# Modulations in column tiles, paired attention heads, and state-space parameters computed inside the mixture, in a whole-model kernel on one core

## The chip, the cores and the metric

One core of a Trainium2 chip runs the whole kernel in one launch. The metric is the device time of an execution in microseconds (us), and the figure given is the median over several executions. The engines are named as in the profile: PE is TensorE (PEld its weight load), DVE is VectorE, ACT is ScalarE, POOL is GpSimd, SP is SyncE, which only issues the transfers of the weights.

## The reference

The input is 256 tokens of width D = 1024, in fp32, and a conditioning vector `c` of D numbers. Everything below is computed in fp32 or in split fp32 products. Cut to what matters here:

```python
# first block, layer 0 (forgetting attention) and layer 1 (latent attention)
c_act = silu(c)
for layer in range(2):
    sh1, sc1, g1, sh2, sc2, g2 = split(c_act @ w_mod[layer] + b_mod[layer], 6)     # 6 x 1024 numbers
    h = rmsnorm(x, g) * (1 + sc1) + sh1
    mix = forgetting_attention(h) if layer == 0 else latent_attention(h, shared_kv)
    x = x + g1 * mix
    h = rmsnorm(x, ffn_norm_g) * (1 + sc2) + sh2
    x = x + g2 * grouped_moe(h)              # 16 experts, 2 of them per token
    if layer == 0: shared_kv = mla_shared_kv(x, c_act, ...)   # with 2 x 1024 modulations of its own
x = rmsnorm(x, final_norm_g)
# forgetting attention: 16 heads of 64
log_f = log_sigmoid(h @ w_f + b_f); cum = cumsum(log_f)
s = q k^T / 8 + cum[query] - cum[key]; p = softmax(causal(s)); o = p v
# second block
xn = rmsnorm(x, norm1_g)
u, q, k, v, qi, ki, wi, g_ssm, g_attn = split(xn @ w_in)
# state space, 32 groups x 64 states, 16 channels a group
dt = exp(log_dt); a_bar = exp(lam * dt); b_bar = (a_bar - 1) / lam * b
state[t] = a_bar * state[t-1] + b_bar u[t];  y = Re(c state) + d_skip * u
y_ssm = gelu(y); y_ssm = y_ssm * sigmoid(y_ssm @ w_glu)
y_attn = attention over the 64 keys with the highest index score (qi, ki, wi) of each query
x = x + (sigmoid(g_ssm) * (y_ssm @ w_ssm_up) + sigmoid(g_attn) * (y_attn @ w_attn_up)) @ w_out
x = x + peer_ffn(rmsnorm(x, norm2_g));  out = rmsnorm(x, norm_f_g)
```

## The kernel before

Each engine has one instruction stream in a fixed order, written out by hand; semaphores tie them together. Tokens lie in two chunks of 128 partitions (`C = 2`). There is no planner; what runs when is the order in which each stream is written.

**Weights.** SP loads the dense weights as slabs of 1024 rows by 512 columns (2 MB) into a ring of three (L505 to L545); the load of slab r waits until slab r-3 is released. `stream` (L172) lists the slabs and cuts them into pieces of at most 512 columns. `gemm` (L727) multiplies one piece after another; `gemm3` (L700) does it for the pieces of `stream_cut`, whose weights ACT and DVE first split into a high and a low part (`highs`, `lows`), three products for each. In the mixture of experts (MoE) the ring holds units of 512 KB, freed by `moe_low`, the count of DVE's low parts.

**Modulations.** `c_act` lies as a column `cT[:, k]` for each of 8 blocks of 128. For a piece of 512 modulations, `gemm` multiplies (L751) the column, broadcast to 128 x 128, with the 128 x 512 weights, 8 times, so that the sum stands on every partition; DVE adds the bias, which lies broadcast in `MOD` (`add_bias`, L1381). The 6144 modulations of layer 0 (`mod0`, 12 pieces) come first in the program, ahead of everything else. Their bias (3 MB broadcast) is loaded on ACT's queue, ahead of X. The modulations of the shared KV and the first two parts of layer 1 are summed on DVE during MoE 0 (`mod_part_of`, L1612, into the accumulators `ACC`), and after it PE adds them over the partitions and adds the bias (L944 to L960), in 32 matmuls of 256 columns, two kinds alternating: one with the bias rows (L956), one with `ones` (L958). Only then is the KV norm's gain loaded by POOL. The other parts of layer 1 (`mod1_a` to `mod1_e`) are `gemm` pieces between the projections.

**Attention A** (L758 to L822 on PE, L1448 on DVE). A step is four heads of one chunk of queries, eight steps in all. For every head PE multiplies q and k (L779, 64 rows) and adds `-cum[key]` with a second matmul of 16 rows (L781, a broadcast column of the identity against `NCT`). DVE adds the mask and takes the maximum, ACT the exponential, DVE normalizes, PE transposes (L794) and multiplies with v (L808).

**State space and attention C.** After layer 1 DVE computes two norms (`rms`, L1351), then the state-space parameters (L1736 to L1795, on 128 x 16 tiles), the powers `POW`, the rotary rotation of the attention C projections (L1797) and the phase tables for b = 0 (`first_phases`, L1804): powers of `a_bar/|a_bar|` for 256 steps, by doubling. The 16 states' tiles are done in four rounds b = 0..3 (L1819 to L1849): PE makes `bu` (L995), DVE rotates by the phases, scans 8 times, and rotates back. POOL makes the phase tables of b = 1, 2, 3 (L613 to L636), those of 2 and 3 after the states of the round two before, as they share two buffers. PE does `c_u` (the u projection), `c_p` (q, k, v, index) and then, between the rounds, `c_g` (four pieces, the gates). The outputs y5 of the state space (L1009, L1011) are taken in token layout: DVE adds `d_skip * u`, ACT does the gelu, PE transposes, then `glu`, the product, and a second transpose. Only after this come the index scores (L1029), the top-64 selection (L1867 to L1888) on DVE, attention C, `ssm_up` and `attn_up`. The small inputs of the state space (27 transfers on POOL's queue, L599 to L610) are issued between layer 1's attention and its experts.

After the merge come the output projection and the product-key experts (PEER), which the change leaves alone.

## Time and profile before

| | before |
|---|---|
| median of 3 runs | 2576.05 us |
| runs | 2576.4, 2576.05, 2563.88 us |
| profiled execution, its own time | 2567.64 us |
| its span | 2565.7 us |
| mean granted clock of PE | 0.862 |
| instructions | 22185 |
| read from memory | 609.69 MB |
| busy share | PE 80%, DVE 58%, PEld 52%, ACT 32%, POOL 24% |

The span runs from the first to the last instruction of the profiled execution; 1.94 us of its time lie outside. A busy share says how long an engine had an instruction under way, not that it set the end. All positions below (as "at 201 us") are from the span's start. In a row of the chain of waits the first number is the start, the second the duration; the chain is the work that ended last, followed back from the last instruction.

### The profile page before, as it was taken

How to read it: one execution, taken by the hardware profiler on the slowest of the kernel's cores; microseconds unless marked ns; L12 is line 12 of the kernel's file. 1: busy time of each engine (PE TensorE's matmuls, PEld its weight loads, DVE VectorE, ACT ScalarE, POOL GpSimd, SP SyncE). 2: the span in 40 equal slices, each digit the busy share in tenths (PEclk: the TensorE clock that was granted, in tenths of full speed). 3: DMA queues.
4: the chain of work that ended last, by engine and by line, in shares of the span. 5: the costliest groups of instructions: out<-in, count | busy, mean ns of one | idle time of the engine just before them, and what ended most of it. 6: DMA issues, size and time to landing. Idle time of an engine off the chain costs nothing.

```text
span 2565.7 us, 22185 instructions
## 1 busy us (share of the span) xinstructions
PE 2052.1 (80%) x7651; PEld 1342.8 (52%) x7651; DVE 1500.0 (58%) x2516; ACT 827.9 (32%) x1266; POOL 611.1 (24%) x749
## 2 busy tenths in 40 slices
PE   5999779999998886999993876488177767677777
PEld 2495568888745665788882444358133223233223
DVE  1243567899843456558994674534675556475642
ACT  0043234588713433447881100223121112121110
POOL 0000000000000003000000363000556666666663
PEclk9995779999979987999997976688588888888788
DMA  8740058999944407669983301031789999999996
GB/s 315 271 166 0 1 206 294 328 388 375 348 156 158 176 33 149 206 204 353 379 334 135 134 20 70 33 131 58 288 334 363 372 381 355 376 372 359 369 382 254
DMA packets 193711, 617.46 MB, mean 241 GB/s; under 512 B 18968, under 2 KB 21328, under 8 KB 193088
## 3 DMA queue, kind: packets, MB, share of 16 engines
q1 hardware_dynamic: 114336, 325.98, 35.3%
q0 software_dynamic: 78704, 285.11, 30.0%
q10 hardware_dynamic: 560, 4.96, 0.5%
q8 instruction: 61, 1.00, 0.2%
q14 instruction: 50, 0.41, 0.0%
HBM read 609.69 MB, written 6.29 MB: 240 GB/s over the span
## 4 chain that ended last, share of the span: by engine, by line
PE 63%; DVE 11%; issue 10%; POOL 7%; DMA 4%; ACT 2%; another core or an unknown queue 1%; SPq 0%; DVEq 0%; ACTq 0%; POOLq 0%
PE PS L882 16%; PE PS L1056 13%; PE PS L903 8%; PE PS L719 5%; PE PS L751 5%; PE PS L738 4%; PE PS L710 4%; POOL peer_rows L654 2%; PE PS L779 2%; POOL peer_rows L665 1%; DVE AR L1326 1%; POOL AR L665 1%; PE PS L781 1%; DVE peer_rows L1963 1%
## 5 line engine op out<-in xcount | busy, mean ns | idle before, releaser
L1963 DVE SCALAR_TENSOR_TENSOR peer_rows<-peer_rows,PS 128x1024 f32<-128x1024 f32 x256 | 311.5, 1217 | 143.5 <-DMA peer_rows<-in_peer_u,MOD 124.1
L1609 DVE TENSOR_TENSOR weights_low<-ring,weights_high 128x1024 fp32r<-128x1024 f32 x231 | 278.9, 1223 | 79.8 <-ACT weights_high L1158 77.3
L1056 PE MATMUL PS<-peer_rows,HT 128*128 128x512 f32 x376 | 193.5, 654 | 125.5 <-ACT HT L1314 77.2
L1158 ACT ACTIVATE weights_high<-ring 128x1024 fp32r<-128x1024 f32 x231 | 242.9, 1061 | 121.2 <-PE PS L882 76.0
L654 POOL DMA_INDIRECT peer_rows<-in_peer_u,MOD x256 | 242.2, 946 | 151.2 <-DVE MOD L1953 73.4
L1609 DVE TENSOR_TENSOR weights_low_more<-ring,weights_high_more 128x1024 fp32r<-128x1024 f32 x153 | 185.3, 1223 | 46.6 <-ACT weights_high_more L1158 44.9
L1056 PEld LDWEIGHTS PS<-peer_rows,HT 128*128 128x128 f32 x376 | 76.5, 208 | 239.5 <-issue 158.7
L1491 DVE TENSOR_TENSOR weights_low<-ring,weights_high 128x1024 fp32r<-128x1024 f32 (+1 forms) x81 | 96.4, 1198 | 158.4 <-ACT weights_high L1080 158.1
L562 POOL DMA_DIRECT2D expert_rows<-HT x10 | 5.4, 543 | 768.2 <-ACT HT L1180 768.2
L1158 ACT ACTIVATE weights_high_more<-ring 128x1024 fp32r<-128x1024 f32 x153 | 161.1, 1061 | 72.2 <-PE PS L882 44.6
L882 PE MATMUL PS<-weights_high,slots_high 128*128 128x512 f32 x386 | 156.2, 405 | 10.1 <-DVE weights_low L1609 10.1
L665 POOL DMA_INDIRECT peer_rows<-in_peer_v,MOD x148 | 140.7, 951 | 88.3 <-issue 37.8
L751 PE MATMUL PS<-ring,cT 128*128 128x512 f32 x320 | 144.4, 613 | 21.6 <-DMA ring<-in_w_mod 20.5
L1080 ACT ACTIVATE weights_high<-ring 128x1024 fp32r<-128x1024 f32 (+1 forms) x81 | 83.1, 1040 | 236.4 <-DMA ring<-in_a_w_in 100.1
L1308 ACT ACTIVATE MOD<-MOD 128x16 f32<-128x16 f32 x16 | 3.4, 216 | 481.5 <-DVE peer_rows L1963 244.3
L882 PE MATMUL PS<-weights_low,slots_high 128*128 128x512 f32 x386 | 154.2, 400 | 0.0
L882 PE MATMUL PS<-weights_high,slots_low 128*128 128x512 f32 x386 | 154.1, 399 | 0.0
L1056 PE MATMUL PS<-AR,HT 128*128 128x512 f32 x216 | 115.8, 672 | 42.7 <-issue 39.5
L1056 PE MATMUL PS<-peer_rows,AR 128*128 128x512 f32 x216 | 113.2, 659 | 45.0 <-issue 42.6
L738 PE MATMUL PS<-ring,HT 128*128 128x512 f32 (+3 forms) x320 | 120.9, 540 | 1.4 <-ACT HT L1071 1.4
L665 POOL DMA_INDIRECT AR<-in_peer_v,MOD x108 | 102.6, 950 | 80.4 <-remote 42.3
L1056 PE MATMUL PS<-AR 128*128 128x512 f32 x216 | 107.2, 645 | 15.8 <-issue 14.0
(356 smaller groups left out, 4077.4 us busy)
## 6 DMA issues: line engine op xcount, KB each, us to landing
ring<-in_exp_w_gate SPq DMA_DIRECT2D x128, 512.0 KB, 5.7
ring<-in_exp_w_up SPq DMA_DIRECT2D x128, 512.0 KB, 5.7
ring<-in_exp_w_down SPq DMA_DIRECT2D x128, 512.0 KB, 5.5
ring<-in_w_mod SPq DMA_DIRECT2D x20, 2048.0 KB, 8.3
ring<-in_w_in SPq DMA_DIRECT2D x7, 2048.0 KB, 8.6
ring<-in_a_w_in SPq DMA_DIRECT2D x6, 2048.0 KB, 7.8
ring<-in_kv_w_mod SPq DMA_DIRECT2D x16, 512.0 KB, 5.0
ring<-in_w_mod SPq DMA_DIRECT2D x16, 512.0 KB, 5.2
```

The costliest lines, as they stand in the source:

```text
L654: pool.indirect_dma_start(out=u_row(k), out_offset=None, in_=A["peer_u_2"][0], in_offset=bass.IndirectOffsetOnAxis(ap=EXPERT[:, c, PT_ * h ...
L665: pool.indirect_dma_start(out=v_row(k), out_offset=None, in_=A["peer_v_2"][0], in_offset=bass.IndirectOffsetOnAxis(ap=EXPERT[:, c, PT_ * h ...
L710: last = nc.tensor.matmul(PS[:, pair + j // 2, o:o + T], ws[a][:, k, :], tokens[b][:, k, :], start=i == 0, stop=i == len(steps) - 1)
L719: last = nc.tensor.matmul(PS[:, pair + c, 0:n], tokens[b][:, 2 * j + k, P * c:P * c + P], ws[a][:, k, :], start=j == 0 and k == 0 and i == ...
L738: last = nc.tensor.matmul(PS[:, pair + c, 0:n], lhs[:, k, P * c:P * c + P], w[:, k, off:off + n], start=k == 0, stop=k == s["kb"] - 1)
L751: last = nc.tensor.matmul(PS[:, pair, 0:n], cT[:, k:k + 1].to_broadcast((P, P)), w[:, k, off:off + n], start=k == 0, stop=k == s["kb"] - 1)
L882: last = nc.tensor.matmul(PS[:, (0 if kind == "G" else 2) + i, :], (XTH, XTL)[b][:, 2 * q + k, P * tile:P * tile + P], w[a][:, DE * k:DE * ...
L903: last = nc.tensor.matmul(PS[:, y_bank(r, ti) + half, :], hidden[b][:, q, P * i:P * i + P], w[a][:, 512 * half:512 * half + 512], start=j ...
L1056: last = nc.tensor.matmul(PS[:, 4 + 2 * c + half, :], diagonal(k), v_row(k)[:, 512 * half:512 * half + 512], start=h == 0 and j == 0, stop ...
L1158: A_(high_of(n0 + n), raw(ring_slot(layer, m)), ACT.Copy).then_inc(S("moe_high"), 1)
L1609: V.tensor_tensor(low_of(n0 + n), raw(ring_slot(layer, ring_no[layer, "E", n])), high_of(n0 + n).bitcast(fp32), ALU.subtract).then_inc(S(" ...
L1963: V.scalar_tensor_tensor(u_row(k), u_row(k), 1.0, PS[:, 2 * c:2 * c + 2, :].rearrange("p a k -> p (a k)"), ALU.mult, ALU.mult, accum_out=D ...
```

## The change

1. **Modulations in column tiles.** The column is broadcast to 128 x 32 only, and the 8 blocks are placed in turn in four column tiles of 32, so that a partial sum of two blocks stands on each quarter of the partitions. ACT copies them to `PARTS` (`mod_copies`), one matmul with `ones` (128 x 128 against 128 x 512) adds them over the partitions, 32-fold, and DVE adds the sum times 1/32 to the bias in `MOD` (`add_mod`). The partial products of piece i+1 are issued ahead of the total of piece i.
2. **Modulations of layer 0 in four parts.** `mod0_a` (4 pieces) and `mod0_b` (1) come before `a_qk`; `mod0_c` (5) after `a_v` and the cumulated sums, before attention A; `mod0_d` (2) after `a_o`. The bias's last 2 MB are loaded by POOL; X comes ahead of the bias on ACT's queue; the statistics of the first norm are taken before the modulations arrive.
3. **Paired heads in attention A.** The forget piece (16 columns) is the first of `a_v`. `Fn`/`NCT` stand twice, at rows 0 and 64, and the bias matmul has 64 rows, in the same half as its head; the order is q·k of the even head, q·k of the odd head, bias even, bias odd, so that successive matmuls alternate between row halves.
4. **Sums after MoE 0.** POOL puts the bias on partition 0 of the accumulators before MoE 0, and PE adds them in 8 matmuls of 512 columns.
5. **State-space parameters in MoE 1.** The same small DVE operations are cut into some 23 steps; one follows each of DVE's expert units from n = 19 on. ACT's exponentials and sines stand at n = 18 and n = 24 of its own units, the first behind a wait for all 27 transfers, which POOL issues once `moe_low` is past 12 units of layer 1. POOL then makes small phase tables (16 steps near, 16 steps far; operations of at most 256 elements a partition), and, after it has gathered the expert rows and the weight stages are free, the full tables of all four b, each of 6 operations on 128 x 1024. `n1`'s gain has a place of its own, `MOD[:, 0:D]`.
6. **State-space order.** `c_u` and `glu` are computed transposed, which takes away three sets of transposes; outputs are 32-column tiles side by side; the skip is a per-partition scalar (`skip`); the rotation stands after round b = 1; the index scores and the top-64 stand ahead of `glu`'s product, and `ssm_up` and the fourth gate piece (`c_h`) ahead of attention C.

```diff
-        gemm("mod0", None, ("c_act", 1))
+        gemm_mod("mod0_a")
+        gemm_mod("mod0_b")
         tp("h_a", ...)
         gemm("a_qk", None)
         gemm("a_v", HT)
...
+        gemm_mod("mod0_c")
         tp("cum", ("negcum", 1))
         attention("A", ...)
         gemm("a_o", None)
+        gemm_mod("mod0_d")
...
+            def partial(g, r, off, n, kind):
+                slab_loaded(pe, r)
...
+                for k in range(DB):
+                    j = 32 * (k % 4)
+                    last = nc.tensor.matmul(PS[j:j + 32, pair_of[g], 0:n], cT[:, k:k + 1].to_broadcast((P, 32)),
+                                            w[:, k, off:off + n], start=k < 4, stop=k >= 4, tile_position=(0, j))
+                last.then_inc(S("mod_partial"), 1)
+            def total(g, r, off, n, kind):
+                pe.wait_ge(S("mod_copied"), mod_no[g] + 1)
...
+                nc.tensor.matmul(PS[:, pair_of[g] + 1, 0:n], ones, PARTS[:, mod_no[g] % 2, 0:n], ...)
...
-                    if a == "A":
-                        last = nc.tensor.matmul(o, ident[0:HEADS, h:h + 1].to_broadcast((HEADS, P)),
-                                                NCT[0:HEADS, 0:kl], start=False, stop=True)
+                    if a == "A" and i % 2:
+                        for x in range(2):
+                            b = slice(64 * x, 64 * x + 64)
+                            last = nc.tensor.matmul(place(i - 1 + x), ident[b, 64 * x + h - 1 + x:64 * x + h + x].to_broadcast((64, P)),
+                                                    NCT[b, 0:kl], start=False, stop=True)
...
+                if layer and n == 18:          # ACT, among the highs of MoE 1
+                    act.wait_ge(S("ssm_in"), 16 * (2 * 2 + 8 * 2 + 6 + 1))
+                    A_(SP_[2], SP_[2], ACT.Exp).then_inc(S("dt"), 1)
...
+                    if n >= 19:                # DVE, among its lows
+                        next(beside, None)
...
+        pool.wait_ge(S("moe_low"), RING_PAST[1] + RUNITS)      # ahead of the 27 small transfers
...
+        expert_rows(1)
+        pool.wait_ge(S("moe_used"), 2 * N_UNITS)
+        bcast(MOD[:, 0:D], gain_list[gain_no["n1"]][1], "gain_in")
+        for b in range(4):
...
+            pool.tensor_tensor(ta, far[0], near[0], ALU.mult)
+            link(pool, pool.tensor_tensor(tb, far[1], near[1], ALU.mult), "pool")
+            link(pool, pool.tensor_tensor(er_, ta, tb, ALU.subtract), "pool")
...
+        inputs(0)
+        gemm("c_p", HT, only=slice(0, 1))
+        inputs(1)
+        gemm("c_p", HT, only=slice(1, 3))
+        outputs(0)
+        inputs(2)
+        gemm("c_g", HT, only=slice(0, 1))
+        outputs(1)
+        gemm("c_g", HT, only=slice(1, 2))
+        inputs(3)
+        outputs(2)
+        gemm("c_g", HT, only=slice(2, 3))
+        outputs(3)
+        tp("qi", ("ropeC", 1), ("y5_pre", 4), evacuated("c_g"))
+        tp("ki")
...
+        index_scores(0)
+        gemm("glu", Y5T, ("y5", 1))
+        index_scores(1)
+        tp("qC", evacuated("glu"))
+        tp("kC")
+        gemm("ssm_up", Y5T, ht("kC"), ("y5g", 1))
+        gemm("c_h", HT)
+        attention("C", [("index_read", 2), evacuated("ssm_up"), evacuated("c_h")])
+        gemm("attn_up", ATT["C"]["O"], ("o", 20))
```

## Rows read from the trace of the kernel before

**Rows 1.** The page: busy times of the engines, then the chain's shares by engine.
```profile
PE 2052.1 (80%) x7651; PEld 1342.8 (52%) x7651; DVE 1500.0 (58%) x2516; ACT 827.9 (32%) x1266; POOL 611.1 (24%) x749
...
PE 63%; DVE 11%; issue 10%; POOL 7%; DMA 4%; ACT 2%; another core or an unknown queue 1%; SPq 0%; DVEq 0%; ACTq 0%; POOLq 0%
```

**Rows 2.** Stretches: us, PE, PEld, DVE, ACT, POOL busy (x), PEclk, DMA share, GB/s.
```profile
26.00:112.00 86.00, 85.78 (x195) 37.90 (x196) 18.14 (x33) 2.95 (x3) 0.59 (x1) 1.00 0.89 313
...
201.00:286.00 85.00, 81.00 (x273) 49.43 (x274) 30.00 (x38) 27.13 (x85) 0.00 (x0) 0.53 0.00 0
...
967.00:1011.00 44.00, 23.40 (x143) 20.84 (x141) 25.88 (x70) 10.24 (x15) 19.10 (x30) 0.74 0.66 73
1399.00:1476.00 77.00, 65.12 (x213) 33.33 (x211) 46.41 (x169) 12.75 (x20) 23.23 (x57) 0.94 0.34 115
1476.00:1590.00 114.00, 75.77 (x272) 46.81 (x272) 79.72 (x82) 4.35 (x4) 61.78 (x113) 0.71 0.14 51
1590.00:1664.00 74.00, 35.39 (x186) 23.84 (x186) 38.31 (x82) 20.92 (x55) 0.00 (x0) 0.62 0.08 29
```

**Rows 3.** The chain of waits, its longest pieces: start us, us, what.
```profile
1.22 24.87 DMA ring<-in_w_mod
26.22 85.70 PE PS L751 x192
120.04 48.28 PE PS L710 x384
...
857.60 13.73 PE PS L751 x32
...
1402.12 44.98 PE PS L738 x128
...
1664.73 27.75 PE PS L738 x64
```

**Rows 4.** The timeline of PE in attentions A, B and C: start, duration, count.
```profile
206.90 1.22 PE L779 MATMUL PS<-AR 64*128 64x256 f32 x2
...
208.05 1.22 PE L781 MATMUL PS<-AR,consts 16*128 16x256 f32 x2
...
888.54 1.97 PE L794 MATMUL PS<-consts,AR 128*128 128x128 f32 x8 [3.15 <-DVE AR L1474]
...
900.13 1.97 PE L794 MATMUL PS<-consts,AR 128*128 128x128 f32 x8 [3.55 <-DVE AR L1474]
...
1651.09 2.08 PE L779 MATMUL PS<-AR 64*128 64x256 f32 x8
```

**Rows 5.** The timeline between MoE 0 and the KV projection, PE and DVE.
```profile
707.34 0.69 PE L956 MATMUL PS<-AR,consts 16*128 16x256 f32 x2
...
730.86 1.22 PE L958 MATMUL PS<-MOD,consts 128*128 128x256 f32 x2
...
737.36 1.23 DVE L1349 SCALAR_TENSOR_TENSOR GAIN<-AR,GAIN 128x1024 f32<-128x1024 f32 x1 [13.45 <-DMA GAIN<-in_kv_norm_g]
```

**Rows 6.** DMA issues from 960 to 1062 us: count, KB each, median us to landing.
```profile
AR<-in_log_dt POOLq DMA_DIRECT2D x2, 4.0 KB, 18.0
```

**Rows 7.** DVE's timeline in the state space: start, duration, what.
```profile
1391.82 1.22 DVE L1357 SCALAR_TENSOR_TENSOR H<-X 128x1024 f32<-128x1024 f32 x1 [4.42 <-DMA GAIN<-in_norm_g]
...
1452.49 2.73 DVE L1326 TENSOR_TENSOR AR<-AR,consts 128x144 f32<-128x144 f32 x4
...
1461.88 1.34 DVE L1326 TENSOR_TENSOR AR<-AR,consts 128x144 f32<-128x144 f32 x4
...
1475.89 1.23 DVE L1829 TENSOR_TENSOR AR<-PS,AR 128x1024 f32<-128x1024 f32 x1
...
1495.18 1.22 DVE L1829 TENSOR_TENSOR AR<-PS,AR 128x1024 f32<-128x1024 f32 x1
...
1528.80 1.23 DVE L1829 TENSOR_TENSOR AR<-PS,AR 128x1024 f32<-128x1024 f32 x1 [13.65 <-POOLq L636]
```

**Rows 8.** POOL's timeline in the phase tables, while DVE waited.
```profile
1516.37 0.61 POOL L633 TENSOR_TENSOR GAIN<-AR 128x256 f32<-128x256 f32 x1
```

More of the change, by code:

```diff
@@ L251, in build @@
         evac_at.append(("evac_" + e, n_by[e]))
-    pair_of = [4 if name == "c_g" else 2 * (g % 2) for g, name in enumerate(pieces)]
+    pair_of = [4 if name in ("c_p", "c_g", "glu", "c_h") else 2 * (g % 2) for g, name in enumerate(pieces)]
+    for i, (g, *_) in enumerate(stages["ssm_up"]):
+        pair_of[g] = 4 + 2 * i
     before = [max((h for h in range(g) if pair_of[h] == pair_of[g]), default=None) for g in range(len(pieces))]
@@ L748, in gemm, with gemm_mod @@
                     continue
-                else:
-                    for k in range(s["kb"]):
-                        last = nc.tensor.matmul(PS[:, pair, 0:n], cT[:, k:k + 1].to_broadcast((P, P)),
-                                                w[:, k, off:off + n], start=k == 0, stop=k == s["kb"] - 1)
                 last.then_inc(S("gemm_done"), 1)
+        def gemm_mod(name):
+            def partial(g, r, off, n, kind):
+                slab_loaded(pe, r)
+                h = before[g]
+                if h in mod_no:
+                    pe.wait_ge(S("mod_copied"), mod_no[h] + 1)
+                elif h is not None:
+                    pe.wait_ge(S(evac_at[h][0]), evac_at[h][1])
+                w = slab_view(r, DB, n)
+                for k in range(DB):
[5 more added lines that the diff above has]
+                pe.wait_ge(S("mod_copied"), mod_no[g] + 1)
+                if before[g] is not None:
+                    pe.wait_ge(S(evac_at[before[g]][0]), evac_at[before[g]][1])
+                nc.tensor.matmul(PS[:, pair_of[g] + 1, 0:n], ones, PARTS[:, mod_no[g] % 2, 0:n], start=True, stop=True
+                                 ).then_inc(S("gemm_done"), 1)
+            for i, piece in enumerate(stages[name]):
+                partial(*piece)
+                if i:
+                    total(*stages[name][i - 1])
+            total(*stages[name][-1])
         def ht(name):
@@ L977, in _ @@
         gemm("b_o", None)
-        gemm("mod1_e", None)
+        gemm_mod("mod1_e")
         tp("h_ffn1", per_chunk=("h_ready", h_no["ffn1"]))
         experts(1)
+        tp("ssm_w", ("ssm_b", 1), *((f"y_out{k}", 2 * OUTS_AT[k]) for k in range(2)))
         tp("h_n1", per_chunk=("h_ready", h_no["n1"]))
         gemm("c_u", HT, ht("h_n1"))
-        gemm("c_p", HT)
-        tp("u", evac_at[stages["c_u"][-1][0]])
-        tp("ssm_w", ("ssm_b", 1))
-        pe.wait_ge(S("tp_out"), tp_end("ssm_w"))
         def inputs(b):
@@ L1098, in evac, with mod_copies @@
             out(len(stages[name]) - 1)
+        def mod_copies(name):
+            for g, r, off, n, kind in stages[name]:
+                m = mod_no[g]
+                act.wait_ge(S("mod_partial"), m + 1)
+                if m >= 2:
+                    act.wait_ge(S("gemm_done"), [h for h in mod_no if mod_no[h] == m - 2][0] + 1)
+                A_(PARTS[:, m % 2, 0:n], PS[:, pair_of[g], 0:n], ACT.Copy).then_inc(S("mod_copied"), 1)
         def to_rows(dst, at=0):
@@ L1208, in _, with v_out @@
         evac("a_qk", qk_out, after="a_v")
-        evac("a_v", lambda i, banks: to_rows(z["V"])(i, banks) if i < 2 else A_(F, banks, ACT.Copy))
+        def v_out(i, banks):
+            if i == 0:
+                return A_(F, banks, ACT.Copy)
+            if i == 1:
+                act.wait_ge(S("f_abs"), 1)
+                A_(Ft, Ft, ACT.Exp, scale=-1.0).then_inc(S("f_exp"), 1)
+                act.wait_ge(S("f_exp"), 1)
+                A_(Ft, Ft, ACT.Ln, bias=ones[:, 0:1]).then_inc(S("f_ln"), 1)
+            return to_rows(z["V"])(i - 1, banks)
+        evac("a_v", v_out)
+        act.wait_ge(S("cum_mm"), 1)
+        cum = PS[:, 7, 0:C * HEADS].rearrange("p (c h) -> p c h", c=C)
+        A_(Fn[:, :, 0:HEADS], cum, ACT.Copy, scale=-1.0)
+        A_(Fn[:, :, 64:64 + HEADS], cum, ACT.Copy, scale=-1.0).then_inc(S("negcum"), 1)
+        mod_copies("mod0_c")
+        tp("cum")
+        highs("a_o", 0, STAGES)
+        attention("A")
+        highs("a_o", STAGES)
+        mod_copies("mod0_d")
         act.wait_ge(S("ang"), 1)
@@ L1660, in _ @@
         wait("small_in", 64)
+        wait("consts_in", 32)
         posf = st[:, 14:16]
@@ L1667, in _ @@
         dve.sem_inc(S("ang"), 1)
-        lows("a_v")
-        wait_evac("a_v")
+        lows("a_v", 0, STAGES + 1)
+        wait(*evac_at[stages["a_v"][0][0]])
         tt(F, F, bf[:, :].rearrange("p (a h) -> p a h", a=1).to_broadcast((P, C, HEADS)), ALU.add)
@@ L1673, in _ @@
         ts(F, F, 0.0, ALU.min)
+        lows("a_v", STAGES + 1)
         wait("f_ln", 1)
         V.tensor_tensor(F, F, Ft, ALU.subtract).then_inc(S("logf"), 1)
+        add_mod0("mod0_c")
         attention("A", out="a_o")
```

487 lines of the change are left out of this document (253 added, 234 removed).

## The prediction

> **What bounds the kernel now.** I began with the page's shares. PE is under way 80% of the span and has 63% of the chain of waits; DVE has 11% of it, POOL 7%, DMA 4% [rows 1]. So it is a PE kernel on average, but such shares hide stages with other bounds, and the change touches four stages, which I read one by one in the table of stretches and in the chain. (1) At the start nothing but modulations runs: 24.87 us for the first slab, then 85.70 us of L751 in one piece, PE busy 85.78 of 86 us, the DMA at 313 GB/s with a share of 0.89: two bounds nearly level [rows 2, 3]. (2) Attention A: PE busy 81 of 85 us at a granted clock of 0.53, that is near the 1.2 GHz level, while DVE is busy for 30: PE sets the pace [rows 2]. (3) After MoE 0 the sums, then DVE waits 13.45 us for a gain [rows 5]. (4) In the state space DVE is the longest chain: 46 of 77 us, then 80 of 114, with waits of 13.65 us on POOL in between, and from 1590 to 1664 nobody is busy for more than 38 of 74 us, a stage of waits [rows 2, 7]. The rest, the two MoEs and PEER, stays. I sum against the profiled execution (2567.64 us, 8.4 below the median of the runs shown); the start of each stage is taken from its rows.
>
> **Start.** Twelve pieces take 85.70, so 7.1 us each; two pieces in a row elsewhere took 13.73, 6.87 each [rows 3]. Each is 8 matmuls of 512 columns, 0.86 apiece. In column tiles, if four run at once, the 8 cost 8/4 x 0.86 = 1.7, with the switch say 2.1; the total with `ones` is one more such matmul, 0.86: 3 us a piece. No row before shows column tiles; the bounds are 6.87 + 0.86 = 7.7 (no overlap) and 2.6, and the row nearest is attention C's, where matmuls in two row halves do overlap (8 instructions of 256 columns in 2.08 us, while attention A's, one after another, need 1.15 for two) [rows 4], so I take 3. Five pieces would then be 15 us of PE, and the transfers decide: before `a_qk` can start, 5 slabs of 2 MB, the first of `a_qk`, X (1 MB), the bias (3 MB) and constants and a gain (1.2) must land, some 17 MB, at 313 GB/s [rows 2] 54 us. With the norm, its transposes and the first splits behind them, `a_qk` starts at about 62 where it started at 120.04 [rows 3]. From there to attention A took 81 us (120.04 to 201) and takes about 96: the cumulated sums and then the five pieces `mod0_c`, whose last slabs are asked for only as earlier ones come free, 5 x 6.7 us of transfer, partly under `a_v`. Attention A starts at 158 instead of 201: **-43** (-50 to -33; the far end is `mod0_c` wholly exposed). The two pieces of `mod0_d`, about 6 us of PE, lie under DVE's product and norm before MoE 0; DVE's two adds cost 1.5: **+1.5**.
>
> The Trainium skill ("TensorE: Matmul & The Clock Gate", Part 3, "Measured speedup vs the span model") gives 2.38 times for three column tiles of 32 at 512 columns. No row of this case shows it; by that the 8 matmuls would be near 2.9 us and the piece 3.8, an estimate from that page, which the transfers at the start would hide.
>
> **Attention A.** The two matmuls of a head start 1.15 us apart at 256 columns [rows 4], so the four heads' scores are 8 x 1.15 = 9.2 us a step, and 5.8 at 128 columns. Attention C's scores have the same 64-row halves in turn, and there 8 instructions (four heads) took 2.08 [rows 4]. With bias matmuls in the same halves, twice that: 4.2. PE drops from 81 to about 50 us, and then DVE and ACT's softmax chain is the bound, as it is in attention B, where PE waits for DVE L1474 at 888.54 and again at 900.13: 11.6 us for a pair of steps [rows 4]; A's have a bias more: 13.4 a pair on average, 4 pairs and the ends, 59 us for 85 [rows 2]: **-26** (-31 if it goes at B's pace, -10 if the 64-row bias matmuls do not pair).
>
> **Between MoE 0 and attention B.** The sums run from 707.34 to the last at 730.86 and 1.1 more, 24.6 us, the gain is asked for behind them, and DVE waits 13.45 [rows 5]. Eight matmuls of 512 columns are 7 at 0.86, up to 11 at the low clock. The gain leads DVE, so **-13.4**. POOL's memsets and four bias rows lie under MoE 0, where POOL only waits for results to store. Of the later pieces, each 6.87 by the chain's 13.73 for two [rows 3], `mod1_b` ends before its DVE step (-4.6, what stood out), `mod1_d` before attention B goes from 13.73 to 6 (-7), `mod1_e` -1.4, a and c hide. Sum **-26** (-30 to -12).
>
> **Start of MoE 1.** From 967 to 1011 the DMAs move 73 GB/s though their share is 0.66: 27 small transfers in small elements lie between the first expert loads [rows 2]. PE idles 20.6 of these 44 us; bounds for what the transfers' leaving gives are 0 and those 20, and since a DVE norm and routing fill most of it, I take a third: -7. They are now issued after 12 units, near 1035, and ACT's 18th unit, near 1054.7, waits for all. A `log_dt` row took 18.0 us to land [rows 6]. They overlap each other before, so all land within 17 to 35 us of the first: a stall of ACT of 0 to 16, of which the units split ahead cover a part: +2. Behind that wait on ACT stand the highs, for which DVE and PE wait, so nothing covers a longer one. DVE's 23 steps of small operations (some 150, at under 0.2 each 25 us in all) stand between lows of which ACT's highs, not DVE, set the pace. **-5** (-8 to +10).
>
> **State space.** Taken away: the wait for the gain, 4.42 [rows 7]; the parameters and powers ahead of the first round; the first phase table on DVE; two waits on POOL of 13.65; the transposes of u, y5 and y5g and the gelu and `glu` between the last round and the index scores. Left on the path: the norm, `c_u` (a third of the 44.98 for it and `c_p`), its evacuation, `bu`, then four rounds of 19.3 (1475.89 to 1495.18) [rows 3, 7], the rotation (24 operations, at 0.335 for 144 elements [rows 7] and in proportion for 320: 13), four skips, keys, index scores, and the two top-64, some 26 us of the 38 for which DVE is busy after 1590 [rows 2].
> Added: POOL's 24 operations of 128 x 1024, at 0.57 for each 256 [rows 8] 2.2 each, 52 us, from the end of MoE 1 on, beside DVE's gated sums and two norms. How they get along is seen in the rotation: four DVE operations of 128x144 took 2.73 us while POOL worked on its tables and 1.34 once it did not [rows 7]. DVE operations with two inputs thus wait for POOL's, one by one. A dozen wide DVE operations lie in the path, so 12 x 2.2 = 26 of the 52 are lost if each alternates with one of POOL's, 36 if the norms' tiny ones are blocked too, 0 if none; I take 26 to 31. The normed tokens, ready at 1399, are then ready near 1421 (-4.4 + 26 or so), the first round starts at 1443 and, with rotation and skips, the last ends near 1534; the index scores of the first chunk follow at 1540, where before the last round's output was only being read near 1590. Then DVE is no longer the bound: PE has `glu` (7, half a piece), `ssm_up` behind y5g, `c_h`, 13.7 each (two pieces are half of the 27.75 [rows 3]), until about 1590; attention C follows to 1620, and only `attn_up`, 13.7, is left: 1634 where it was 1692.5. **-58** (-92 without any conflict, -40).
>
> The Trainium skill ("SBUF — State Buffer", "SBUF: two separate sides") says of the port that GpSimd and VectorE share: an "exclusive lock, not a bandwidth split", held for the whole instruction, also by DVE operations with two inputs. The rotation's rows agree in kind; by that rule every two-input DVE operation, tiny ones too, waits for a whole 2.2, and the stage would give -52 instead of -58.
>
> **Sum.** -43 + 1.5 - 26 - 26 - 5 - 58 = -156.5: 2567.6 - 156.5 = **2411 us**. Its own range is 2375 to 2450.
>
> **Rivals.**
> A. The column tiles don't overlap: 7.7 us a piece. Five pieces 38 us, still under the transfers but with a tail (+10), `mod0_c` +7, `mod0_d` +8 exposed, mod1 pieces dearer than before instead of cheaper (+15): **2451**. For it: no row shows them; against it, row halves overlap in this kernel [rows 4].
> B. POOL's 52 us come first and DVE gives way wholly, or PE, now with `ssm_up` and `c_h` ahead of attention C, ends as late as before: the state space gives 10 instead of 58: **2459**. For it: the port rows; against it, 114 us of stretch with 34 idle on DVE.
> C. No conflict at all (the tables land between DVE operations), attention A at B's pace: -34 and -5 more: **2372**.
> D. The other side: the 27 small transfers, now under the full weight stream, land one after another. ACT's stream stands at n = 18 until the last, and no expert weight is split meanwhile. At 18 us each [rows 6] that is 486 less the 19 of lead: +467, less 156: **2879**. It turns the sum when each costs over (156 + 19)/27 = 6.5 us. Against it: the rows of 4 KB transfers before landed in 8 to 18 us though 27 were under way, so they overlapped.
> E. It does not do what it says: the softmax chain in A was PE's clock and not its work, and the start is held by transfers that the order does not shorten (24 MB of `w_mod` still have to come, now between others): start and attention give 25 together instead of 68: **2454**.
>
> **Chances.** The forecast 0.64, A 0.08, B 0.10, C 0.06, D 0.04, E 0.08. All but D are faster by over 0.5% (13 us, about what a measurement of this kernel can tell from no change). Some mishaps together could bring it to level: faster 0.93, same 0.02, slower 0.05. The range takes in A, B and C: 2368 to 2465.
>
> **What would show it.** Right: attention A starting at 155 to 162; DVE, not PE, as the releaser in it; the groups of L751's successor at under 2.5 us per 8 matmuls; no wait for the KV gain; ACT not idle at its 18th unit; POOL's 24 operations at 2 to 2.5 us with DVE's norm stretched beside them; index scores near 1540 less the 98 won earlier. Wrong: partial sums at 0.86 a matmul; a long idle time of ACT in MoE 1 released by a DMA; DVE waiting on phases in all rounds.

## The result and the profile after

The changed kernel takes 2432.73 us (median of 4, 2423.04 to 2435.07), the kernel before 2572.19 (median of 4, 2563.88 to 2576.4): a ratio of 0.9454, 95% interval 0.9416 to 0.9493, so 139 us less. The forecast was 2411, 22 us too low, with 2432.73 inside its range and inside the likeliest case's own. The profiled execution took 2430.41, its span is 2428.6, against 2565.7: 137.1 less where the sum said 156.5.

The page of the changed kernel, busy times and then the chain's shares by engine; beside [rows 1] PE's share of the chain fell from 63% to 54%:

```profile
PE 1899.5 (78%) x7603; PEld 1263.4 (52%) x7603; DVE 1520.8 (63%) x2470; ACT 838.3 (35%) x1283; POOL 603.4 (25%) x638
...
PE 54%; issue 14%; DVE 12%; POOL 8%; DMA 8%; ACT 3%; another core or an unknown queue 1%; SPq 0%; DVEq 0%; ACTq 0%; POOLq 0%
```

Stretches of the changed kernel, columns as in [rows 2]:

```profile
0.00:26.00 26.00, 5.19 (x33) 1.27 (x33) 4.68 (x18) 2.37 (x4) 3.65 (x9) 1.00 0.95 327
26.00:61.00 35.00, 16.36 (x82) 4.89 (x75) 16.77 (x17) 7.28 (x11) 1.13 (x2) 0.79 1.04 395
61.00:156.00 95.00, 91.09 (x612) 75.39 (x614) 31.36 (x39) 34.59 (x40) 0.00 (x0) 0.95 0.59 208
156.00:210.00 54.00, 34.68 (x272) 27.17 (x272) 29.27 (x37) 27.07 (x84) 0.00 (x0) 0.75 0.21 76
868.00:913.00 45.00, 29.67 (x142) 26.70 (x143) 30.42 (x76) 14.13 (x19) 0.00 (x0) 0.63 0.37 140
913.00:1276.00 363.00, 348.58 (x1536) 282.78 (x1536) 272.94 (x325) 226.74 (x244) 35.97 (x59) 0.98 0.83 278
1289.00:1347.00 58.00, 1.01 (x5) 1.01 (x6) 56.81 (x39) 0.00 (x0) 53.61 (x22) 0.50 0.00 1
1366.00:1460.00 94.00, 85.64 (x308) 40.75 (x304) 86.75 (x107) 6.64 (x7) 0.00 (x0) 0.94 0.33 116
```

In the first 61 us PE is busy for 21.6 and the DMAs for all of it: the start is bound by transfers. Attention A is the stretch from 156 to 210, with PE busy 35 of 54 where it was 81 of 85 [rows 2]. From 1289 to 1347 DVE runs 39 instructions in 56.8 us while POOL runs 22 in 53.6; that is the norm.

Where each stage starts in the two traces (us from the span's start; the end of MoE 1 is the end of its last matmul, behind which the changed kernel also transposes weights of the state space):

| from ... to | before | after | change | forecast |
|---|---|---|---|---|
| start to attention A's first scores | 201.14 | 155.85 | -45.3 | -43 |
| (in it: start to `a_qk`) | 120.04 | 61.01 | -59.0 | -58 |
| attention A, to `a_o` | 285.85 | 210.20 | -30.4 | -26 |
| to the first expert weights of MoE 0 | 359.11 | 287.04 | +3.6 | +1.5 |
| MoE 0, to the sums | 707.34 | 635.49 | +0.2 | 0 |
| sums, KV, attention B, to the norm's transposes | 967.24 | 870.01 | -25.4 | -26 |
| to the first expert weights of MoE 1 | 1011.75 | 913.00 | -1.5 | -7 |
| MoE 1, to its end | 1358.6 | 1272.8 | +12.9 | +2 |
| to `c_u` | 1402.12 | 1350.35 | +34.1 | } -58 |
| `c_u` to the output projection | 1704.11 | 1567.67 | -84.7 | } |
| output projection and PEER, to the end | 2565.7 | 2428.6 | -0.7 | 0 |

PE and DVE in the changed kernel for the first half of the table, from the timeline: two modulation pieces, the four score groups of an attention step at 256 columns, the sums after MoE 0, and DVE's first use of the KV gain (against [rows 3 to 5]):

```profile
40.34 3.27 PE L796 MATMUL PS<-ring,cT 128*32 128x512 f32 x16 [5.95 <-DMA ring<-in_w_mod]
...
151.19 1.92 PE L796 MATMUL PS<-ring,cT 128*32 128x512 f32 x16 [0.91 <-DMA ring<-in_w_mod]
...
196.12 0.97 PE L840 MATMUL PS<-AR 64*128 64x256 f32 x4
196.93 0.59 PE L844 MATMUL PS<-AR,consts 64*128 64x256 f32 x4
197.36 0.59 PE L840 MATMUL PS<-AR 64*128 64x256 f32 x4
197.79 0.59 PE L844 MATMUL PS<-AR,consts 64*128 64x256 f32 x4
...
204.55 1.97 PE L857 MATMUL PS<-consts,AR 128*128 128x128 f32 x8 [4.51 <-DVE AR L1584]
...
637.20 3.60 PE L1020 MATMUL PS<-AR,consts 128*128 128x512 f32 x8
...
652.22 1.23 DVE L1452 SCALAR_TENSOR_TENSOR GAIN<-AR,GAIN 128x1024 f32<-128x1024 f32 x1
```

A piece's 8 partial matmuls (16 instructions, each matmul showing as two) take 1.92 us against 6.87 at the full granted clock, and 3.27 in the first row above, where the granted clock was 0.58; either waits for its slab. The eight score matmuls of a step run from 196.12 to the transposes at 198.31, 2.2 us against 9.2 [rows 4] (the granted clock in the two stretches is 0.86 and 0.50), and what PE then waits for is DVE's normalization (4.51 us). The gain of the KV norm is there: no wait stands behind L1452, where 13.45 us stood [rows 5].

PE's first matmul with expert weights of MoE 1, before and after, and in the kernel before the wait of ACT and the stretch ahead of it:

```profile
1011.75 0.77 PE L882 MATMUL PS<-weights_high,slots_high 128*128 128x512 f32 x1 [8.48 <-DVE weights_low L1609]
...
1009.22 1.06 ACT L1158 ACTIVATE weights_high<-ring 128x1024 fp32r<-128x1024 f32 x1 [8.40 <-DMA ring<-in_exp_w_gate]
...
987.00:1000.00 13.00, 12.08 (x61) 10.47 (x62) 6.29 (x9) 4.94 (x7) 0.00 (x0) 0.83 0.95 17
```
```profile
913.00 0.77 PE L945 MATMUL PS<-weights_high,slots_high 128*128 128x512 f32 x1 [1.62 <-DVE weights_low L1792]
```

Second half. What ACT waited for at its 18th unit of MoE 1, how long the small transfers took to land, from 935 to 985 us, PE's longest wait in MoE 1 (waiting line, releaser: total us, times, longest), and what PE does behind its last matmul:

```profile
975.52 0.22 ACT L1268 ACTIVATE AR<-AR 128x16 f32<-128x16 f32 x1 [19.88 <-DMA AR<-in_d_skip]
```
```profile
AR<-in_a_re POOLq DMA_DIRECT2D x2, 4.0 KB, 9.3
AR<-in_a_im POOLq DMA_DIRECT2D x2, 4.0 KB, 11.6
AR<-in_log_dt POOLq DMA_DIRECT2D x2, 4.0 KB, 17.2
AR<-in_d_skip POOLq DMA_DIRECT2D x1, 2.0 KB, 21.9
```
```profile
PE PS L966 <- DVE weights_low L1792: 10.8, 1, 10.8
```
```profile
1272.39 0.40 PE L966 MATMUL PS<-weights_low_more,hidden_high 128*128 128x512 f32 x1
1273.95 1.94 PE L725 MATMUL PS<-consts,AR 128*128 128x128 f32 x16 [1.16 <-issue]
```

The norm between MoE 1 and `c_u`, grouped by line and form over 1289 to 1347 us (busy us, mean ns); the last three rows are the norm's own operations, on 2 elements a partition and on 1024:

```profile
L668 POOL TENSOR_TENSOR phases_all<-phase_tmp 128x1024 f32<-128x1024 f32 x4 | 12.2, 3038 | 0.3
...
L1429 DVE TENSOR_TENSOR st<-st 128x2 f32<-128x2 f32 x6 | 6.4, 1063 | 0.2
L1446 DVE SCALAR_TENSOR_TENSOR st<-st 128x2 f32<-128x2 f32 x6 | 6.3, 1048 | 0.2
...
L1458 DVE SCALAR_TENSOR_TENSOR H<-X 128x1024 f32<-128x1024 f32 x2 | 6.3, 3138 | 0.0
```

The same groups in the kernel before, over 1375 to 1399.2 us:

```profile
L1359 DVE SCALAR_TENSOR_TENSOR H<-X 128x1024 f32<-128x1024 f32 x2 | 2.4, 1220 | 0.0
...
L1343 DVE SCALAR_TENSOR_TENSOR st<-st 128x2 f32<-128x2 f32 x6 | 1.0, 161 | 0.2
...
L1326 DVE TENSOR_TENSOR st<-st 128x2 f32<-128x2 f32 x6 | 1.0, 161 | 0.2
```

An operation of 0.16 us has become one of 1.05 on average: in the timeline one in two takes 1.8 to 2.2, the next 0.16. From DVE's first sum to the normed tokens pass 58.4 us (1288.78 to 1347.13) against 19.5 before (1375.16 to 1399.09, less the wait of 4.42). POOL is slowed too: its 24 operations take 59.7 us (1284.35 to 1344.01), where 12 of them take 25.3 with DVE out of the way (1310.53 to 1335.83 in the run with the tables behind the norm). Behind the normed tokens DVE has only PE to wait for:

```profile
1366.87 1.23 DVE L1959 TENSOR_TENSOR AR<-PS,phases_all 128x1024 f32<-128x1024 f32 x1 [19.74 <-PE PS L1054]
```

That is the first operation of the first state-space round, 19.7 us behind the normed tokens; before it came 76.8 us behind them (1399.09 to 1475.89 [rows 7]), with the parameters, the powers, the rotation and the first table between.

### The profile page after: what moved, and what is told of

Its sections match the earlier page's. It is cut to its first block, busy times and chain, and to the rows that moved or that the text cites. A ratio compares the mean times of both kernels' runs of the same rounds, so it can differ in the third digit from the quotient of the medians.

```text
span 2428.6 us, 22022 instructions
## 1 busy us (share of the span) xinstructions
PE 1899.5 (78%) x7603; PEld 1263.4 (52%) x7603; DVE 1520.8 (63%) x2470; ACT 838.3 (35%) x1283; POOL 603.4 (25%) x638
## 4 chain that ended last, share of the span: by engine, by line
PE 54%; issue 14%; DVE 12%; POOL 8%; DMA 8%; ACT 3%; another core or an unknown queue 1%; SPq 0%; DVEq 0%; ACTq 0%; POOLq 0%
PE PS L945 15%; PE PS L1129 10%; PE PS L966 7%; PE PS L752 6%; PE PS L771 4%; POOL peer_rows L687 4%; PE PS L743 4%; POOL peer_rows L698 2%; POOL AR L698 2%; DMA peer_rows<-in_peer_u,MOD 2%; DVE AR L1429 1%; DMA ring<-in_w_mod 1%; PE PS L915 1%; DMA peer_rows<-in_peer_v,MOD 1%
## 5 line engine op out<-in xcount | busy, mean ns | idle before, releaser
L1129 PE MATMUL PS<-peer_rows,HT 128*128 128x512 f32 x376 | 198.8, 667 | 126.3 <-issue 123.5
L1129 PE MATMUL PS<-peer_rows,AR 128*128 128x512 f32 x216 | 111.3, 660 | 38.9 <-issue 38.9
L1129 PE MATMUL PS<-AR,HT 128*128 128x512 f32 x216 | 110.8, 650 | 33.5 <-issue 30.8
L771 PE MATMUL PS<-ring,HT 128*128 128x512 f32 (+3 forms) x288 | 104.8, 525 | 2.2 <-ACT AR L1185 1.2
L945 PE MATMUL PS<-weights_high_more,slots_high 128*128 128x512 f32 x254 | 100.4, 395 | 0.0
```

The lines of the kernel that those rows point to most:

```text
L771: last = nc.tensor.matmul(PS[:, pair + c, 0:n], lhs[:, k, P * c:P * c + P], w[:, k, off:off + n], start=k == 0, stop=k == s["kb"] - 1)
L945: last = nc.tensor.matmul(PS[:, (0 if kind == "G" else 2) + i, :], (XTH, XTL)[b][:, 2 * q + k, P * tile:P * tile + P], w[a][:, DE * k:DE * ...
L1129: last = nc.tensor.matmul(PS[:, 4 + 2 * c + half, :], diagonal(k), v_row(k)[:, 512 * half:512 * half + 512], start=h == 0 and j == 0, stop ...
```

## The experiments

They ran in three groups, each on one chip with the kernel before beside it, which took 2504.95, 2499.85 and 2561.7 us there. Differences are taken within a group, ratios to the kernel before across them. The chip of the first two groups grants PE a higher clock (0.89 for the kernel before, against 0.86 in the third group and in the result); of the 70 us between the changed kernel's traces there (2359) and here (2429) nearly all arise in PEER, where the clock behind 1700 us is 0.94 against 0.82.

**The base, and the wait on ACT** (first group). Base:

> The changed kernel itself, unaltered, as the base of the comparisons on this chip. Theory: ratio 0.945 to the kernel before (its interval was 0.942 to 0.949), that is about 137 us less; ACT idle for 19.9 us at its 18th unit of the second mixture, PE's second mixture 16 us longer than the first.

2359.57 us, ratio 0.9419 (0.9406 to 0.9432); ACT idle 20.38 us at its 18th unit. The other three differ in that wait.

```diff
-                if layer and n == 18:
+                if layer and n == 26:
-                if layer and n == 24:
+                if layer and n == 32:
-                    if n >= 19:
+                    if n >= 27:
```

> ACT's wait for the small state-space transfers is moved from its 18th to its 26th unit, the sines from the 24th to the 32nd, DVE's parameter steps from the 19th to the 27th. Theory 1 (the wait of 19.9 us on ACT set the end of this stretch, 16 us on PE): PE's second mixture takes 347 us as the first, the whole 14 to 16 us less than the changed kernel. Theory 2 (the units were late for another reason, a slow transfer of weights beside the small ones): the idle time moves to the weights, and the whole changes by less than 4 us.

```diff
-                    act.wait_ge(S("ssm_in"), 16 * (2 * 2 + 8 * 2 + 6 + 1))
+                    act.wait_ge(S("ssm_in"), 16 * (2 * 2 + 8 * 2 + 6))
...
-        pool.dma_start(DSKIP, ...).then_inc(S("ssm_in"), 16)
+        pool.dma_start(DSKIP, ...).then_inc(S("dskip_in"), 16)
```

> The added transfer of d_skip counts on a semaphore of its own, for which DVE waits at the skip; ACT waits for the other 26. Theory 1 (the 27th transfer, in single numbers, is the slow one that ACT waited for): 14 us less. Theory 2 (the small transfers land one after another, some 2 us apart, and log_dt landed just before it): 1 to 2 us less, ACT still idle for over 17 us, now released by log_dt.

```diff
-        pool.wait_ge(S("moe_low"), RING_PAST[1] + RUNITS)
         for x, (b_, c_) in enumerate((("b_re_2", "c_re_2"), ("b_im_2", "c_im_2"))):
...
+        pool.wait_ge(S("moe_low"), RING_PAST[1] + RUNITS)
         pool.dma_start(DSKIP, ...).then_inc(S("dskip_in"), 16)
```

> The 26 small transfers (all but d_skip, which has a wait of its own) are issued between layer 1's attention and its experts, as in the kernel before; ACT's wait stays at its 18th unit. Theory 1 (they cost the first expert loads nothing or little; only the wait on ACT costs): 14 to 16 us less than the changed kernel, PE idle before the second mixture longer by at most 2. Theory 2 (my prediction's 7 us): the wait is gone but the first expert weights come 7 us later: 8 to 9 us less.

| | median us | against the base | ratio to before |
|---|---|---|---|
| late wait | 2346.68 | -12.9 | 0.9368 (0.9355 to 0.9381) |
| d_skip's own wait | 2361.48 | +1.9 | 0.9430 (0.9417 to 0.9443) |
| small transfers early | 2345.70 | -13.9 | 0.9367 (0.9354 to 0.9380) |

ACT's exponential in the three traces, in this order:

```profile
979.65 0.21 ACT L1268 ACTIVATE AR<-AR 128x16 f32<-128x16 f32 x1
```
```profile
974.24 0.22 ACT L1268 ACTIVATE AR<-AR 128x16 f32<-128x16 f32 x1 [19.09 <-DMA AR<-in_log_dt]
```
```profile
953.66 0.22 ACT L1268 ACTIVATE AR<-AR 128x16 f32<-128x16 f32 x1
```

Theory 1 holds for the late wait and the early transfers: the wait is worth 13 to 14 us, a little less than the 14 to 16 expected. In the traces MoE 1 takes 347.0 us with the late wait and 346.7 with the early transfers, where it takes 360.0 in the base, 359.8 in the changed kernel and 346.9 in the kernel before. It falls for d_skip: the 27th transfer is only the last of a row, and without it ACT waits for the 26th, 1.3 us less (19.09 for 20.38); that moves nothing.

The early transfers cost the first expert loads nothing that can be seen: from the norm's transposes to the first expert weights 42.3 us (868.96 to 911.26), against 43.0 in the base, and PE waits 1.62 us for the weights in both. But they are not back where they were. Here the last is issued at 880.0, 13 us ahead of the first expert load (893.04), which lands after 11.6 us; in the kernel before the last is issued at 985.57, 1.3 us ahead of it (986.85), and it lands after 22.3; without them it lands after 4.3. So this run does not say what moving them away was worth; the waits of 8.48 and 1.62 above do.

**The tables and c_h** (second group).

> The changed kernel again, as the base for the three kernels run beside it. Every theory: ratio to the kernel before 0.942 to 0.949; the two norms after the second mixture take 58 us in the trace, where they took 24 in the kernel before, as POOL's 24 table operations stand beside them.

2362.24 us, ratio 0.9451 (0.9437 to 0.9464), the norm 58 us.

```diff
+        pool.wait_ge(S("h_ready"), C * h_no["n1"])
         for b in range(4):
             near, far = ...
```

> POOL starts its 24 full table operations (52 us in all) only when DVE has written the normed tokens. Theory 1 (DVE and POOL exclude each other for whole instructions, tiny ones too, 34 us lost on the norms): the normed tokens are ready 34 us earlier; the next 20 us, in which DVE waits for PE, hide ten of POOL's operations, and the other 14 delay the state-space rounds by up to 28 us, so that the whole is 6 to 20 us shorter. Theory 2 (the norms were slow for another reason, such as the reads of the gathered rows): ready no earlier than before and the tables late, so 20 us and more longer.

2343.52 us, 18.7 less, ratio 0.9376 (0.9362 to 0.9389). Theory 1, near its far end. The normed tokens are ready at 1310.5, 36 us earlier than in the base, and POOL's first ten operations or so fall in DVE's wait for PE. Then the same exclusion shows in the scans of the first round, DVE's timeline:

```profile
1332.19 1.23 DVE L1960 TENSOR_TENSOR AR<-PS,phases_all 128x1024 f32<-128x1024 f32 x1 [21.74 <-PE PS L1055]
1336.84 2.18 DVE L1430 TENSOR_TENSOR AR<-AR 128x1024 f32<-128x1024 f32 x1
...
1341.92 2.72 DVE L1969 TENSOR_TENSOR_SCAN scans<-AR 128x256 f32<-128x256 f32 x1
1344.56 2.35 DVE L1970 TENSOR_TENSOR_SCAN scans<-AR 128x256 f32<-128x256 f32 x1
```

A scan takes 0.67 us alone. The first row, which reads PSUM and one table, keeps its 1.23 beside a POOL operation under way.

```diff
-            pool.tensor_tensor(ta, far[0], near[0], ALU.mult)
...
+            V.tensor_tensor(ta, far[0], near[0], ALU.mult)
...
+        phase_table(0)
+        phase_table(1)
...
+            if b >= 2:
+                phase_table(b)
```

> DVE itself makes the full tables, 24 operations of 1.22 us: those of b = 0 and 1 behind the norm, where it waits 19.7 us for PE, those of b = 2 and 3 ahead of their rounds; POOL only makes the small ones. Theory 1 (exclusion of whole instructions): normed tokens 34 us earlier, 14.6 us of tables hidden, 14.6 exposed, in a stage that ends PE-bound on c_h: 20 to 30 us less in all. Theory 2 (no exclusion, the tables cost DVE nothing on POOL): 15 us more.

2338.12 us, 24.1 less, ratio 0.936 (0.9347 to 0.9373). Theory 1 again. DVE's timeline:

```profile
1305.72 2.48 DVE L1458 SCALAR_TENSOR_TENSOR H<-X,st,MOD 128x1024 f32<-128x1024 f32 x2
1308.42 1.23 DVE L1943 TENSOR_TENSOR phase_tmp<-MOD 128x1024 f32<-128x1024 f32 x1 [0.21 <-DVE H L1458]
...
1329.79 1.23 DVE L1965 TENSOR_TENSOR AR<-PS,phases_all 128x1024 f32<-128x1024 f32 x1 [6.80 <-PE PS L1042]
```

The norm takes 19.7 us again (1288.55 to 1308.2), 29 us of work on DVE cost less than 60 us on POOL beside it, and after two tables DVE still waits 6.80 for PE.

```diff
-        gemm("ssm_up", Y5T, ht("kC"), ("y5g", 1))
-        gemm("c_h", HT)
+        gemm("c_h", HT, ht("kC"))
+        gemm("ssm_up", Y5T, ("y5g", 1))
```

> The fourth gate piece stands ahead of ssm_up (in the stream of the weights, on PE and on ACT), where PE otherwise idles 6 us for the product y5g. Theory 1 (from the last index scores on, PE sets the end of attention C's start: DVE waits 22 us for its first scores): 6 us less. Theory 2 (the slab of ssm_up now comes too late, or attention C's chain has slack): no difference, within 2 us.

2357.99 us, 4.3 less, ratio 0.9436 (0.9423 to 0.9449): the two intervals overlap, so this is not settled, though in the traces the way from `c_u` to `peer_q` is 2.7 us shorter (253.7 against 256.4).

**The parts of the first half, and all improvements together** (third group). Here the base is the ratio of the two groups before, 0.9419 and 0.9451, mean 0.9435; 0.001 is 2.6 us. The two differ by 8 us for the same kernel, a little beyond their intervals, and stand for another chip here, so differences of under some 10 us can't be told in this group.

```diff
-                    last = nc.tensor.matmul(PS[j:j + 32, pair_of[g], 0:n], cT[:, k:k + 1].to_broadcast((P, 32)),
-                                            w[:, k, off:off + n], start=k < 4, stop=k >= 4, tile_position=(0, j))
+                    last = nc.tensor.matmul(PS[:, pair_of[g], 0:n], cT[:, k:k + 1].to_broadcast((P, P)),
+                                            w[:, k, off:off + n], start=k == 0, stop=k == DB - 1)
```

> Only the column tiles are undone: each of the 8 matmuls of a modulation piece uses the column broadcast to 128 x 128 and the whole array, copies, the total with ones and the order of the pieces stay. Theory 1 (tiles cut a piece's 8 matmuls from 6.87 to 1.9 at the full clock, and PE is near the pace of the transfers at the start): a_qk starts 10 us later, mod0_c shows 19 us more, mod0_d 8, the pieces of layer 1 about 15 in all: 45 to 55 us more than the changed kernel, ratio to the kernel before 0.962 to 0.967. Theory 2 (the start and mod0_c are bound by transfers, and the gain is the order's alone): 15 us more at most, ratio 0.951 or less.

2465.41 us, ratio 0.9621 (0.9594 to 0.9649): 48 us more. Theory 1. In the chain `a_qk` starts 9 us later than in the changed kernel, and pairs of pieces of 13.8 us stand in it, where a pair took 5.6:

```profile
70.11 48.85 PE PS L743 x384
...
144.87 13.83 PE PS L795 x32
...
260.98 13.75 PE PS L795 x32
```

```diff
-                    if a == "A" and i % 2:
-                        for x in range(2):
+                    if a == "A":
+                        for x in (i % 2,):
                             b = slice(64 * x, 64 * x + 64)
-                            last = nc.tensor.matmul(place(i - 1 + x), ident[b, 64 * x + h - 1 + x:64 * x + h + x].to_broadcast((64, P)),
+                            last = nc.tensor.matmul(place(i), ident[b, 64 * x + h:64 * x + h + 1].to_broadcast((64, P)),
```

> In attention A each head's bias matmul follows its own q k product, so that two matmuls in the same row half stand one after the other; rows, sizes and everything else as in the changed kernel. Theory 1 (only matmuls that alternate between row halves overlap): the pairs q k and bias serialize within a half, PE's scores cost about twice as much (4.2 to 8 us a step), and with the softmax chain of DVE and ACT behind them attention A takes 65 to 80 us instead of 54: 11 to 25 us more. Theory 2 (the chain of DVE and ACT has the slack to hide it, or neighbours overlap all the same): up to 4 us more.

2423.43 us, ratio 0.9458 (0.9431 to 0.9485): no difference that can be told. Theory 2, in its second form. Attention A takes 54.3 us (156.22 to 210.49), as in the changed kernel (54.4), and PE's scores of a 128-column step run at the same pace in both; first unpaired, then the changed kernel:

```profile
176.51 0.50 PE L840 MATMUL PS<-AR 64*128 64x128 f32 x4
176.84 0.40 PE L844 MATMUL PS<-AR,consts 64*128 64x128 f32 x4
```
```profile
176.17 0.49 PE L840 MATMUL PS<-AR 64*128 64x128 f32 x4
176.50 0.39 PE L844 MATMUL PS<-AR,consts 64*128 64x128 f32 x4
```

The x4 says more. A matmul shows as two instructions, and in the unpaired program each q·k is followed by its own bias; still four instructions of L840 stand together, those of two heads, and in the single records the two heads' q·k start 13 ns apart (7 ns in the changed kernel). So the two row halves run beside one another in either order, and this run never had them one behind the other, which it was meant to try. In the kernel before, with all bias matmuls on rows 0 to 15, L779 and L781 stand by two and start 1.15 us apart [rows 4]. Writing the order in pairs is not what made attention A faster. What remains of the edit is the bias matmul: its size, 64 rows for 16, and its place in the half of its head; neither was tried by itself.

```diff
         gemm_mod("mod0_b")
+        gemm_mod("mod0_c")
+        gemm_mod("mod0_d")
         tp("h_a", per_chunk=("h_ready", h_no["a"]))
...
-        gemm_mod("mod0_c")
         tp("cum", ("negcum", 1))
...
-        gemm_mod("mod0_d")
```

> All 12 pieces of layer 0's modulations stand ahead of a_qk as in the kernel before, but in column tiles. Theory 1 (transfers bound the start: 7 more slabs at 6.3 us each in front of a_qk, and 19 us of mod0_c and 4 of mod0_d less later): 18 to 25 us more than the changed kernel, a_qk starts near 105. Theory 2 (the tiles alone made the gain at the start): within 5 us.

2442.67 us, ratio 0.9535 (0.9508 to 0.9563): 26 us more. Theory 1 (18 to 25), and by the traces 20: `a_qk` starts at 101.91, 41 us later, and the first expert weights of MoE 0 are reached at 307.16 instead of 287.04.

> The later wait on ACT, the tables on DVE and c_h ahead of ssm_up together. They measured 12.9, 24.1 and 4.3 us less than the changed kernel each by itself. Theory 1 (three places one behind the other on the path): the sum, 41 us less than the changed kernel, ratio to the kernel before 0.927 to 0.930. Theory 2 (with the tables on DVE the rounds of the state space end later than PE's part, so that c_h's place no longer matters, or the late parameters delay the small tables): 30 to 37 us less.

2384.29 us, ratio 0.9295 (0.9272 to 0.9318), the fastest version: 36 us less than the changed kernel by the mean ratio, 177 less than the kernel before beside it. The ratio lies in the range of theory 1, the difference in that of theory 2; the interval of 12 us holds both, and the base is no surer than that. In the chains `peer_q` starts 36.1 us earlier than in the base of the second group (1569.51 against 1605.65).

## Why the prediction was right, and where it was off

**Start, forecast -43, measured -45.3.** The transfers decide it, as the sum had it: `a_qk` at 61.0 for 62. Tiles and order both count and neither alone would do. With tiles but all pieces in front `a_qk` starts at 102; with the order but without tiles at 70, and attention A at 184.5 for 155.9, because `mod0_c` is then PE's 7.7 us a piece and not the transfers' 6. The price of the tiles is confirmed: 1.92 for my 2.1, and 2.8 a piece in all for my 3 where two follow one another (3.64 and 1.98 us for `mod0_d`'s two). Rival A (no overlap, +40) would have been a good estimate of what the tiles are worth: 48 without them.

The figure of the Trainium skill's page "TensorE: Matmul & The Clock Gate" (Part 3, "Measured speedup vs the span model", 2.38 times) is for three column tiles; taken for these four it would have made the 8 matmuls 2.9 us, an estimate. The trace says 6.87/1.92 = 3.6 times for four tiles at 512 columns; the measurement decides.

**Attention A, forecast -26, measured -30.4.** The end is right: the bound passes from PE to the softmax chain, PE busy 35 of 54 us. So is the price of overlapping halves: 4.2 us a step at attention C's granted clock of 0.50 are 2.4 at the 0.86 of the changed kernel's step, and 2.2 were measured; the sum had not counted on the higher clock. Wrong was what makes them overlap. I had it that the program must alternate between the halves, with -10 if the bias matmuls do not pair; the unpaired order overlaps as well and costs nothing that can be told. Which part of the new bias matmul did it stays open.

**Between, forecast -26, measured -25.4.** The sums take 7.0 us (635.49 to 642.51), the gain's 13.45 are gone. No run undid either by itself.

**MoE 1, forecast -5, measured +11.4 (-1.5 and +12.9), outside the step's own range of -8 to +10. This is the step that failed**, and in one of its two terms.

"+2" for ACT's wait was mis-sized: it measured 12.9 by the trace, 13 to 14 by the runs. The issue of the transfers (24 us behind the first expert weights) and ACT's 18th unit (43 us) came where the sum had them. The landing did not: I had all of them land within 17 to 35 us of the first issue, so a stall of 0 to 16; the last landed 38 us after it, and ACT stalled for 19.9, of which the units split ahead covered 7, where my +2 needed nearly all. I had read "18.0 us to land" [rows 6] as a time that the transfers share. The first twenty, of 16 and 64 KB, do land 3 to 5 us after their issue. The last seven, of 2 and 4 KB in 4-byte elements and issued 0.8 us apart, fall behind one another: 5.3, 6.0, 12.9, 13.2, 17.3, 21.5 and 21.9 us to landing. The kernel before shows the same row, 3.0 us for the first of its six and 23.8 for the last. And they hold up the weights behind them: a slab issued at 953.82 landed 22.0 us later.

"-7" for the first expert loads was a bare third of PE's idle time, but the size was right: PE's wait for the first expert weights fell from 8.48 us to 1.62, 6.9 less. In the kernel before ACT waits 8.40 for the first slab, while the DMAs are 95% busy at 17 GB/s; the slab and the last small transfer land together (1009.20 and 1009.34). That the whole stretch is only 1.5 us shorter has other reasons, which the sum did not see. `mod1_e` is short now, so PE is ready ahead of the norm: its transposes start with the first chunk and wait for the second, and the router's matmuls behind them take 6.98 us at a granted clock of 0.50, where they took 3.72 at 1.00, close behind `mod1_e`'s unbroken full-width matmuls. (The kernel before has 26 small transfers, not 27; `d_skip`'s was added.)

The rival D had the mechanism with a price of 18 apiece; the last seven came at about 3.6, all 27 at 1.4 (38 us), far from the 6.5 at which it would have turned the sum.

**State space, forecast -58, measured -50.6.** `c_u` starts 34 us later behind MoE 1's end, where I took 22, and the stretch behind it is 85 us shorter. Of these, 57 lie between the normed tokens and the first round (19.7 us for 76.8), where the parameters, the rotation and the first table stood; the rest I put down to the new order, and no run took these apart. The norm lost 38.9 us (58.4 against 19.5) beside POOL's 59.7, where I took 26 to 31. By the rule of the Trainium skill's page "SBUF — State Buffer" ("SBUF: two separate sides": an exclusive lock for the whole instruction) the prediction had estimated -52. The trace agrees, down to the operations of 2 elements, and I should have taken it whole. That the end of the stretch is PE's, with c_h before attention C, shows in DVE's wait of 22.15 us for the first scores (1515.20). Rival C (no conflict) is excluded by the two table runs, B by the 50 us that the stage did win and by DVE's rounds, which once the tables are done run at 19.3 to 19.7 us each; E by the start and attention A, which won 72 us together.

So the sum was right within its own range, with a little luck: MoE 1 is 16 us off and the state space 7, the other steps together 4 the other way, most of it attention A's unforeseen clock, which together is the 19.4 between sum and result. ACT's stall and the norm's loss were both taken from within wide bounds where the trace before (23.8 us to landing for the last small transfer) and the lock's rule said more.

## What to carry to other kernels

Small transfers in 4-byte elements on one queue can land one after another, and hold up larger ones behind them: put the wait well behind the last issue (here the last landed 22 us after it), or issue them in a stretch where nothing depends on them; here either is worth 13 to 14 us. Work given to POOL beside a chain of small DVE operations is not free: about one in two of them waits for a whole POOL instruction, and tables that take POOL some 51 us alone, and 60 there, cost DVE 39, where DVE itself needs 29, of which 15 fall in a wait. For a matmul whose stationary operand is one broadcast column, four column tiles and one summing matmul take 2.8 us of PE for 6.9, at the full granted clock.

## What the runs showed of the hardware

- Four column tiles of 32 at 512 columns: 1.92 us for 8 fp32 matmuls that took 6.87 in full width, both at a granted clock of 1.00.
- DVE operations on 2 elements, 0.16 us alone, took 1.76 to 2.19, about every second of them, beside POOL operations of two inputs, which took up to 4.3 us for 1.9 to 2.3; scans 2.3 to 2.7 for 0.67; an operation that reads PSUM and one SBUF tensor kept its 1.23.
- Matmuls of 64 rows in the two row halves overlapped whether the program alternates between the halves or not: two heads' q·k start 7 to 13 ns apart in both. Eight at 256 columns took 2.2 us at a granted clock of 0.86; in turn with matmuls of 16 rows it was 9.2 [rows 4] at 0.50. The clock is 1.7 of these 4.2 times.
- Seven transfers of 2 and 4 KB, issued 0.8 us apart on POOL's queue, took from 5.3 to 21.9 us to land; a 512 KB slab issued behind them took 22.0, and 22.3 in the kernel before, where it takes 4.3 without them.
